# Moving the last five cache copies of a layer between two page gathers, in a one-core decoder kernel

## The reference

```python
def trunk_layer(x, pos, past, keep, l, P):
    h = rmsnorm(x, P['n_f1_pre'][l])
    x = x + 0.5 * rmsnorm(swiglu(h, P['f1_wg'][l], P['f1_wu'][l], P['f1_wd'][l]), P['n_f1_post'][l])
    h = rmsnorm(x, P['n_mix_pre'][l])
    mixed, new_state = token_mixing(h, pos, past, keep, l, P)
    x = x + rmsnorm(mixed, P['n_mix_post'][l])
    h = rmsnorm(x, P['n_f2_pre'][l])
    x = x + 0.5 * rmsnorm(swiglu(h, P['f2_wg'][l], P['f2_wu'][l], P['f2_wd'][l]), P['n_f2_post'][l])
    return x, new_state
# in token_mixing:
    m = (gates[:, :, 0] * (ya @ P['w_branch_a'][l]) + gates[:, :, 1] * (yb @ P['w_branch_b'][l])
         + gates[:, :, 2] * (yc @ P['w_branch_c'][l]))
    new_state = dict(ckv=ckv, krope=krope, swa_k=k_all[:, -keep:], swa_v=v_all[:, -keep:],
                     wkv=wkv_new, shift=shift_new)
# in reference, the sample group's past rows are read through the page table:
                      ckv=cache_mla_ckv[l][page_table].reshape(db, past_len, KV_LORA),
                      krope=cache_mla_krope[l][page_table].reshape(db, past_len, DROPE))
```

## Time and profile before

| | |
|---|---|
| median of three executions | 2620.01 us (2619.12 to 2623.54) |
| the profiled execution | 2631.68 us |
| its span, first to last instruction | 2629.9 us |
| TensorE (PE) busy | 97% of the span |
| VectorE (DVE), ScalarE (ACT), GpSimd (POOL) busy | 50%, 21%, 3% |
| mean granted TensorE clock | 0.989 |
| data moved by DMA | 505.66 MB |

### The profile page before, as it was taken

One profiled execution on the slowest core, in us unless ns is written; L12 is line 12 of the kernel. 1 busy time (PEld: TensorE's weight loads), 2 busy tenths in 40 slices (PEclk: granted clock), 3 DMA queues, 4 the chain that ended last, 5 costly groups with the idle time before them and its releaser, 6 DMA issues.

```text
span 2629.9 us, 52961 instructions
## 1 busy us (share of the span) xinstructions
PE 2547.6 (97%) x23108; PEld 2065.5 (79%) x23108; DVE 1314.0 (50%) x2847; ACT 560.4 (21%) x1249; POOL 67.3 (3%) x92
## 2 busy tenths in 40 slices
PE   7999999999999999999999999999999998999998
PEld 6999856656666667999999998566666666689998
DVE  4663553335543372656366545533455334627654
ACT  2110231123422221311021102311344222221010
POOL 0000000000000110000000000000000001100000
PEclk9999999999999899999999999999999998999999
DMA  6444678543962469443554456685439433794443
GB/s 229 144 116 143 222 243 321 210 149 129 384 255 81 148 222 371 140 149 102 142 165 129 121 154 242 241 319 194 173 140 389 183 120 143 272 332 146 130 111 86
DMA packets 260549, 505.66 MB, mean 192 GB/s; under 512 B 9760, under 2 KB 198560, under 8 KB 245216
## 3 DMA queue, kind: packets, MB, share of 16 engines
q1 hardware_dynamic: 251616, 330.83, 38.1%
q0 software_dynamic: 8704, 171.45, 17.7%
HBM read 491.95 MB, written 140.85 MB: 241 GB/s over the span
## 4 chain that ended last, share of the span: by engine, by line
PE 92%; DVE 2%; DMA 2%; ACT 2%; issue 1%; PEld 0%; SPq 0%; DVEq 0%
PE ps L716 86%; PE ps L719 5%; DMA big<-in_cache_swa_k_dram 1%; DMA ring<-in_f_wu_dram 1%; PEld ps L716 0%; DVE reg L2012 0%; ACT big L1844 0%; ACT reg L1844 0%; DVE x L2004 0%; SPq L580 0%; DVE reg L2589 0%; DVE ring L2510 0%; DVE reg L2560 0%; DVE reg L2076 0%; SPq L586 0%
## 5 line engine op out<-in xcount | busy, mean ns | idle before, releaser
L716 PE MATMUL ps<-reg 128*128 128x160 f32 (+12 forms) x4584 | 513.8, 292 | 2.5 <-issue 1.6
L716 PEld LDWEIGHTS ps<-reg 128*128 128x128 f32 (+5 forms) x4584 | 454.5, 163 | 34.7 <-issue 25.4
L716 PE MATMUL ps<-h,ring 128*128 128x320 f32 (+2 forms) x1984 | 450.5, 379 | 16.3 <-DMA ring<-in_f_wu_dram 13.5
L716 PE MATMUL ps<-reg,ring 128*128 128x160 f32 (+1 forms) x3040 | 458.9, 306 | 0.0
L716 PEld LDWEIGHTS ps<-reg,ring 128*128 128x128 f32 x3040 | 426.2, 190 | 16.4 <-issue 6.1
L716 PEld LDWEIGHTS ps<-h,ring 128*128 128x128 f32 (+1 forms) x1984 | 324.2, 190 | 106.9 <-issue 29.0
L716 PE MATMUL ps<-ring,h 128*128 128x512 f32 (+3 forms) x896 | 250.7, 472 | 2.0 <-issue 2.0
L716 PE MATMUL ps<-big,ring 128*128 128x160 f32 (+2 forms) x2016 | 216.8, 281 | 7.0 <-issue 6.5
L716 PEld LDWEIGHTS ps<-big,ring 128*128 128x128 f32 (+2 forms) x2016 | 198.7, 169 | 31.2 <-issue 26.9
L716 PEld LDWEIGHTS ps<-ring,h 128*128 128x128 f32 (+1 forms) x896 | 102.2, 163 | 79.1 <-issue 63.7
L716 PE MATMUL ps<-big,reg 32*64 32x256 f32 (+8 forms) x2144 | 143.5, 363 | 4.1 <-issue 4.0
(11 more groups left out here) (320 smaller groups left out, 2645.2 us busy)
## 6 DMA issues: line engine op xcount, KB each, us to landing
out_o_swa_k_s_dram<-in_cache_swa_k_dram POOLq DMA_DIRECT2D x16, 4080.0 KB, 15.6
out_o_swa_v_s_dram<-in_cache_swa_v_dram POOLq DMA_DIRECT2D x16, 4080.0 KB, 16.9
ring<-in_w_in_dram SPq DMA_DIRECT2D x30, 2048.0 KB, 8.7
ring<-in_f_wd_dram SPq DMA_DIRECT2D x32, 1408.0 KB, 7.0
ring<-in_f_wg_dram SPq DMA_DIRECT2D x42, 1024.0 KB, 5.5
ring<-in_f_wu_dram SPq DMA_DIRECT2D x42, 1024.0 KB, 8.1
big<-in_cache_swa_k_dram SPq DMA_DIRECT2D x32, 1024.0 KB, 8.3
ring<-in_cache_swa_v_dram SPq DMA_DIRECT2D x32, 1024.0 KB, 7.5
```

Source lines behind the costliest of these rows:

```text
L716: return pe.matmul(out, lhsT, rhs, start=first, stop=last, skip_group_check=True)
```

## The change

Three edits that don't depend on one another.

1. On POOL the last five copies of each layer move from behind gather 7 to between gather 0 and gather 1.
2. The constants that are needed first (132 columns) are a transfer of their own; the other 5,108 columns are issued after the weights of the next two blocks. VectorE's page row numbers wait on the engine's own step counter in place of `s_index`.
3. At the very end ScalarE multiplies the right half by the norm's weight while the sum of squares is pending, VectorE does two wide multiplications and two wide additions, and the output of the right half goes out in two transfers.

```diff
@@ CONST
+CONST_FIRST = CONST["ident"][0]
@@ sync
-            sp.dma_start(cst[:, :], io["consts"]).then_inc(s_const, 16)
+            sp.dma_start(cst[:, 0:CONST_FIRST], io["consts"][:, 0:CONST_FIRST]).then_inc(s_const, 16)
             for u in range(1, HEAD):
                 first_weights(0, u)
+            sp.dma_start(cst[:, CONST_FIRST:], io["consts"][:, CONST_FIRST:]).then_inc(s_rest, 16)
...
-            for half in range(2):
-                sp.wait_ge(S["x"], ADDED["f2"] + 4 * half + 4)
-                sp.dma_start(io["yT"][:, :, HALVES[half]], x[:, :, HALVES[half]]).then_inc(s_out, 16)
-            sp.wait_ge(s_out, N_ROWS_OUT + 32)
+            for done, half, tiles in ((4, HALVES[0], slice(0, KD)), (6, HALVES[1], slice(0, 4)), (8, HALVES[1], slice(4, KD))):
+                sp.wait_ge(S["x"], ADDED["f2"] + done)
+                sp.dma_start(io["yT"][:, tiles, half], x[:, tiles, half]).then_inc(s_out, 16)
+            sp.wait_ge(s_out, N_ROWS_OUT + 48)
@@ gpsimd
                     elif b == 1:
+                        copied(COPY_AT[1], 2 * NB)
                         pool.wait_ge(S["prompt_mm"], 2 * H + 16)
                         pool.wait_ge(S["ml_prep"], 1)
...
-                copied(COPY_AT[1], 2 * NB)
                 pool.wait_ge(s_copy, l * (16 * 2 * NB) + TABLE + 16 * 2 * NB)
@@ scalar
+            def weighted(f, tiles):
+
+                for k in tiles:
+                    act.activation(yt[:, k, HALVES[1]], yt[:, k, HALVES[1]], ACT.Copy, scale=pp(f + "_post", k))
+
...
+                if tag is None:
+                    weighted(f, (0, 1, 2, 3, 4, 5, 7))
                 act.wait_ge(S["gu_sum"], 5 * n + EC12_)
                 down_square(2 * p, right)
+                if tag is None:
+                    weighted(f, (6,))
                 post_root(f, 1)
@@ vector
+            def last_residual():
+
+                right = HALVES[1]
+                fours = (slice(0, 4), slice(4, KD))
+                wide = rstd[:, right].unsqueeze(1).to_broadcast([P, 4, HT])
+                done = [counted(dve.tensor_tensor(yt[:, four, right], yt[:, four, right], wide, ALU.mult)) for four in fours]
+                for four, after in zip(fours, done):
+                    dve.wait_ge(s_dve, after)
+                    dve.tensor_tensor(x[:, four, right], x[:, four, right], yt[:, four, right], ALU.add).then_inc(S["x"], 2)
...
-                ffn_residual(f, 1, range(4))
+                if tag:
+                    ffn_residual(f, 1, range(4))
+                else:
+                    last_residual()
```

More of the change, by code:

```diff
@@ L55 @@
 _at = 0
-for _n, _w in [("ident", P), ("ones", P), ("onesblk", P), ("reset", T), ("cosb", 24), ("sinb", 24), ("cosc", 48),
-               ("sinc", 48), ("bmask", 4), ("ist", 64), ("pdiv", 1), ("m8p", 64), ("m8Tp", 64), ("o16T", 64), ("o32T", 64), ("o64T", 64),
+for _n, _w in [("ones", P), ("eps", 3), ("pdiv", 1), ("ident", P), ("onesblk", P), ("reset", T), ("cosb", 24), ("sinb", 24), ("cosc", 48),
+               ("sinc", 48), ("bmask", 4), ("ist", 64), ("m8p", 64), ("m8Tp", 64), ("o16T", 64), ("o32T", 64), ("o64T", 64),
                ("sTp", 64), ("iTp", 64), ("sTs", 64), ("iTs", 64), ("swp", 2 * 3 * SEQ),
-               ("mlp", 2 * SEQ), ("sws", SW_COLS), ("mls", TS), ("eps", 3)]:
+               ("mlp", 2 * SEQ), ("sws", SW_COLS), ("mls", TS)]:
     CONST[_n] = (_at, _w)
@@ L427, in build @@
         s_once, s_arrive, s_go, s_pad = sem("constants_in"), sem("engines_at_layer_end"), sem("layer_begun"), sem("pad")
-        s_index = sem("page_rows")
         s_ql = sem("queries_spread")
-        s_const, s_next = sem("constants"), sem("next_params")
+        s_const, s_rest, s_next = sem("first_constants"), sem("other_constants"), sem("next_params")
         s_head = [sem(f"first_weights_{i}") for i in range(HEAD)]
@@ L952, in rwkv @@
             def rwkv():
+                if l == 0:
+                    pe.wait_ge(s_rest, 16)
                 fill(FILL[0])
@@ L1941, in page_rows @@
                     dve.wait_ge(s_copy, TABLE)
-                    dve.tensor_scalar(pidf[:, 0:NB], ptab[:, :], 8.0, C("pdiv"), ALU.mult, ALU.add).then_inc(s_index, 1)
-                    dve.wait_ge(s_index, 1)
+                    link(dve.tensor_scalar(pidf[:, 0:NB], ptab[:, :], 8.0, C("pdiv"), ALU.mult, ALU.add))
                     for half in range(2):
                         q = dve.tensor_scalar(pidf[:, NB * (half + 1):NB * (half + 2)], pidf[:, 0:NB], 2.0, float(half), ALU.mult, ALU.add)
-                    q.then_inc(s_index, 1)
-                    dve.wait_ge(s_index, 2)
+                    link(q)
                 dve.tensor_copy(pidx[:, :], pidf[:, :]).then_inc(S["pages_ready"], 1)
@@ L2250, in rwkv @@
             def rwkv():
+                if l == 0:
+                    dve.wait_ge(s_rest, 16)
                 dve.wait_ge(s_par, 16 * 4)
```

## The result

The changed kernel takes 2639.4 us in the median of 7 runs (2631.54 to 2645.49), the kernel before 2620.7 (7 runs, 2619.12 to 2623.54). The ratio is 1.0065 (estimated from all runs; the two medians alone give 1.0071), with a 95% interval of 1.0047 to 1.0084, which is 12 to 22 us slower. The forecast was 2636.

A forecast was written before the change was run, and what follows sets the result against it. TensorE, busy for 97% of the span, was taken as the bound. 16.2 + 6.8 - 5.5 - 0.7 - 1.2 = +15.6 us on the median of 2620.0 gave about 2636 us; range 2616 to 2646, likeliest case 2628 to 2642.

The forecast's parts named there:

- The mechanism: At gate tile 16 of both layers: pg 4 lands behind the fifth copy, TensorE waits, then its clock drops; 16.2 + 6.8 us.
- The rival that rested on it: At gate tile 16: pg 4 lands in time, before 850 us, so no wait; -7.4 us in sum; chance 0.18.
- pg 4's lateness: At gate tile 16: the load lands 8.9 us late in layer 0, 7.3 in layer 1, together 16.2 us.
- The rule that carried the step: Weight loads beside copies land near the end of the copy issued after them; for pg 4 858.9 us, needed at 850.02.
- Moves mostly in the pause, doesn't quite finish in it: A load beside copies moves mostly between two copies; its last pieces trickle in behind the next; three took 21.1 to 32.9 us.
- The clock: Behind each wait at gate tile 16 TensorE runs at half speed for a while: 3.4 us each, 6.8 us together.
- The old place: Last block of layer 0's sample attention: removing the copies behind gather 7 gives back 5.5 us; nothing in layer 1.
- The start: Engines' meeting at 33.91 us: weights come sooner, TensorE arrives last, -0.7 us; bounds 0 and 2 to 3 us.
- The end: Final norm and output: VectorE 0.8 us less, chain starting 0.6 later, last transfer 1.0 shorter; together -1.2 us.
- The sum: Whole kernel: 16.2 + 6.8 - 5.5 - 0.7 - 1.2 = +15.6 us, about 2636 us.

The follow-up runs named there:

- no_pg4: Changed kernel without the load of pg 4 in either layer, gate tiles 16 to 19 using pg 3's weights; 0.9959 of the kernel before.
- fourth_held: Changed kernel with the fourth moved copy issued only when gate tile 15 is done, when pg 4 is issued; 0.9964 of the kernel before.
- last_two_small: Changed kernel with only the fourth and fifth moved copies in pieces of 8,160 bytes in place of 65,280; 0.9974 of the kernel before.
- small_pieces: Changed kernel with all five moved copies of each layer in pieces of 8,160 bytes in place of 65,280; 0.9958 of the kernel before.
- copies_only: Kernel before with only the five copies of each layer moved between gathers 0 and 1, start and end as before; 1.0059 of the kernel before.
- changed_again: The changed kernel, unaltered, timed once more beside later variants; 1.0066 of the kernel before.
- ends_only: Changed kernel with the five copies back behind gather 7, keeping the edits of start and end; 0.9985 of the kernel before.
- four_and_one_timed: Changed kernel with the fourth copy held until four tiles of branch b are done, the fifth until gate tile 19; 0.9964 of the kernel before.

## Why the prediction was right, and where its sizes were not

**The mechanism** of the loss was right in every step: the five copies run from 769 us on, pg 4 takes 20 us or more, TensorE waits at gate tile 16 of both layers, and the clock is at half speed behind the wait. no_pg4 shows that the load carries the loss, fourth_held and last_two_small that it is the piece sizes and the moment, not the bytes. The rule of the Trainium skill ("DMA: Bandwidth & Descriptors", Queues, rings and completion order), by which an engine drains a whole packet of some 9 to 17 descriptors from one queue before it turns to the next, does not hold in this trace: in the last round of the fourth copy 16 engines took 16 records of the load, one each on average, and in small_pieces 406 of 418 records of the load are followed directly by one of the copy. The rival that rested on it falls with it.

**pg 4's lateness**: 8.9 + 7.3 = 16.2 us predicted, 6.8 + 9.6 = 16.4 measured. The sum was right, its parts not. In layer 0 the fifth copy was issued at 836.25, 6.2 us earlier than I had it: 5.0 as gather 0 came that much earlier, 1.1 as the four periods took 67.3 us in place of 68.4. Gate tile 16 was due at 846.6, only 3.4 us earlier than in the earlier trace rows, and the load landed 17.1 us behind the copy, not 16.5: 8.9 - 6.2 + 3.4 + 0.6 = 6.7. In layer 1 the landing came 18.8 us behind the copy, which adds 2.3 us. The rule that carried the step, a landing near the end of the next copy, held in both. (One sentence of the prediction is too strong: of the three loads that it rests on one had landed 0.8 us before the end of the next copy, at 422.9 against 423.7; this changes nothing in the sum.)

**"Moves mostly in the pause, doesn't quite finish in it"** was inferred from three landings. The records now show it: 59 of 1,024 left at 838 us, as the fifth copy's first pieces run. Why it doesn't finish was not in the prediction: it had no number for what moves beside a copy (nothing for 6.2 us, then 16 records in 3.5 us).

**The clock**: 6.8 us predicted, 2.0 + 1.9 = 3.9 measured. The half-speed stretch began while TensorE still stood idle: in layer 0 the granted clock is down from 850.6 us, 2.8 us before the matmuls go on (over the wait, 846.59 to 853.38, it is 0.79), and only what is left behind the wait costs. Two other executions with the wait lost more in the same way: over 6 us behind each wait the granted clock was 0.50 and 0.57 in copies_only and 0.51 and 0.64 in changed_again, which is 5.6 and 5.1 us for the two. The term was mis-sized, as I counted a whole stretch for each wait.

**The old place** was to give back 5.5 us. This term is the one that the runs don't bear out at its size. It came from one wait in layer 0, which the first line shows. In ends_only, where the copies stand where they stood, the late block of instructions is there again, at the same point of the same group of matmuls (the program runs some 9 us earlier there), but it is 0.94 us long and the clock stays up (977 to 986 us):

```profile
993.63 0.70 PE L716 MATMUL ps<-big,reg 32*64 32x256 f32 x4 [2.59 <-issue]
```

```profile
982.84 0.45 PE L717 MATMUL ps<-big,reg 32*64 32x256 f32 x4 [0.94 <-issue]
...
977.00:986.00 9.00, 8.06 (x172) 5.97 (x173) 3.31 (x15) 1.72 (x5) 0.54 (x1) 1.00 1.17 452
```

So that trace shows 0.9 us in place of 5.5. In the changed kernel nothing waits there (TensorE is busy for 30.00 us from 976 to 1006). The timed runs leave the size open: the variants with all five copies between the gathers and no long wait (no_pg4 0.9959, fourth_held and four_and_one_timed 0.9964) lie 0.21 to 0.26%, 5 to 7 us, below ends_only with 0.9985, which would fit the 5.5, but the intervals overlap.

**The start**: -0.7 predicted, with -2 to -3 as the bound. The same 16 matmuls behind the meeting start at 37.93 in place of 39.99 us: -2.1. The bound's condition came true, the clock stayed up behind the shorter wait: two matmuls took 1.36 us in the earlier trace rows, eight take 2.39 now. This term was mis-sized; I should have taken the bound.

**The end**: -1.2 predicted, some -1.8 measured. VectorE gained 1.0 (0.8 predicted), the last transfer 1.0 (1.0), and ScalarE's seven multiplications delayed the last square by 0.24 us only (0.6): they take 2.33 us together, 0.33 each where I took 0.37, and TensorE's wait before its last sum is 1.17 us where it was 0.93.

**The sum** by the terms of this profile, with the old place at the 0.9 us of ends_only, is 16.4 + 3.9 - 2.1 - 1.8 - 0.9 = +15.5 us. The timed ratio gives +12 to +22 us. The two profiled executions differ by 8.0 us only; there the wait at 991 is in the one and not in the other, and 16.4 + 3.9 - 2.1 - 1.8 - 5.5 = 10.9. The remaining -2.9 us is not taken apart: waits for instructions and half-speed stretches stand at other places in the two. The two parts measured alone, 1.0059 and 0.9985, give 1.0044 together, a little less than the whole; with their own uncertainty (some 0.0026) the difference is not a finding. ends_only's 0.9985 is -3.9 us, which is the sum of start and end, though its interval reaches from -8.4 to +0.3. That the total of 2636 came so near 2639.4 was in part luck: if the old place gave back 0.9 and not 5.5, these 4.6 us were met by 4.7 us of errors the other way, in the clock (2.9), the start (1.4) and the end (0.6), less 0.2 in the wait.

**A better version.** fourth_held and four_and_one_timed, both at 0.9964, and small_pieces, at 0.9958, are faster than both kernels, by some 9 to 11 us than the one before. Their intervals overlap; I would take four_and_one_timed, whose loads have time to spare in both layers; in fourth_held and small_pieces one lands within 0.4 us of its use.

## What to carry to other kernels

A transfer's margin is that of the traffic beside it: 12 us of slack for a load of 7.8 us was not enough once the other queue carried large pieces, since the queues took turns record by record. Before a long copy is moved into a quiet stretch, list the loads issued in it, with the moment each can start at the earliest and the moment it is needed, and tie the copy to the event that starts the load, or better to one well after it. A wait seen in one profiled execution tells where time can be gained, not how much: the same wait had 2.59 us and a half-speed stretch in one trace, and 0.94 us and none in another.

## What the hardware showed that I had not expected

- Two queues shared the DMA engines one record for one record, whatever their sizes: 418 to 418 (2,048 and 8,160 bytes), 16 to 16 (2,048 and 65,280 bytes). The load's share of bytes in such a stretch is set by the size of the other queue's pieces.
- A load issued in the middle of a copy did not begin at once: its first record came 6.2 us after the issue in changed_again and 4.4 us in the changed kernel's profile, against 1.0 us in the kernel before.
- The end of the pause is a cliff: 6.4 us in the issue of a copy (4.2 measured from the load's issue) decide between a wait of 0.20 and one of 10.36 us.
- Waits for instructions moved about between executions of nearly the same program: 24.8 us in 25 places before, 21.3 in 24 after, 12.6 in 19 (ends_only), 8.5 in 9 (changed_again). Cutting all copies small left 10.9 in 11, so the size of the pieces is not what sets them. The cause was not found.
- The level of one and the same kernel differed between the three sets of runs by more than any edit here: 2621.9, 2593.0 and 2590.6 us. They ran on three chips; whether the chip is the reason was not tested.
